# The 32 whole value rows of the second tile, spread among its 96 partial ones

## The reference

```python
cand_idx = i_top[..., 0, :, None] * PEER_KEYS + i_top[..., 1, None, :]   # expert = first key * 128 + second key
best, pos = lax.top_k(cand, PEER_TOPK)          # 16 experts for each of 8 heads and each token
act = gelu(einsum('ckd,cd->ck', expert_u[idx], xc))
out = einsum('ck,ckd->cd', gate * act, expert_v[idx])   # 128 value rows for each token, summed with weights
return rms_norm(h + out, final_norm)
```

## Time and profile before

| | us |
|---|---|
| timed runs | 2013.01, 2016.02, 2017.6 |
| span of the profiled execution, first to last instruction | 2008.7 |
| time around the span in that execution | not in the trace |
| PE, DVE, POOL busy | 1770.1, 1368.9, 1040.7 |
| mean DMA rate over the span | 322 GB/s |

### The profile page before, as it was taken

How to read it: one execution, slowest core, us unless ns; L and a number is a source line. 1 busy time by engine, 2 the same in 40 slices (tenths; PEclk the granted TensorE clock), 3 DMA queues, 4 the chain that set the end, 5 groups by cost and what they waited for, 6 DMA issues and landing times.

```text
span 2008.7 us, 18796 instructions
## 1 busy us (share of the span) xinstructions
PE 1770.1 (88%) x6283; PEld 1122.4 (56%) x6283; DVE 1368.9 (68%) x2191; ACT 574.5 (29%) x1037; POOL 1040.7 (52%) x643
## 2 busy tenths in 40 slices
PE   7999999999999999875565578898887899999996
PEld 6888888888888898622222233344333554444442
DVE  5463453233334338999889887787888888888956
ACT  5445464345543520210111132233313740000001
POOL 5443343444332413575555565465555668877732
PEclk9999999999999999887778899999998899999999
DMA  8986454665555679999999999999999999999997
GB/s 211 241 177 148 142 189 152 192 196 180 169 164 173 204 263 403 384 411 420 418 419 417 402 420 419 414 413 414 403 415 391 401 369 408 409 414 386 409 421 308
DMA packets 157641, 647.28 MB, mean 322 GB/s; under 512 B 25894, under 2 KB 31086, under 8 KB 95598
## 3 DMA queue, kind: packets, MB, share of 16 engines
q0 software_dynamic: 73728, 450.98, 55.2%
q1 hardware_dynamic: 83824, 195.16, 30.9%
HBM read 729.91 MB, written 2.10 MB: 364 GB/s over the span
## 4 chain that ended last, share of the span: by engine, by line
PE 52%; DMA 18%; DVE 13%; issue 9%; POOL 7%; POOLq 0%; ACT 0%; DVEq 0%; SPq 0%; ACTq 0%
DMA u_ring<-in_peer_u_dram,idx 10%; PE acc L1583 10%; PE acc L1585 10%; PE acc L1584 10%; PE misc L1967 8%; PE acc L1967 8%; DMA u_high<-in_peer_u_dram,idx 3%; DVE u_ring L1425 3%; DMA u_mid<-in_peer_u_dram,idx 3%; DVE u_ring L1423 3%; POOL u_ring L595 3%; POOL v_high L602 1%; POOL u_mid L595 1%; DVE u_mid L1425 1%; DVE u_mid L1423 1%
## 5 line engine op out<-in xcount | busy, mean ns | idle before, releaser
L553 POOL TENSOR_TENSOR w_lo<-raw,w_hi 128x1024 fp32r<-128x1024 f32 x112 | 276.3, 2467 | 421.0 <-ACT w_hi L677 420.7
L1583 PE MATMUL acc<-w_hi,t_hi 128*128 128x512 f32 x896 | 355.0, 396 | 0.0
L1585 PE MATMUL acc<-w_hi,t_lo 128*128 128x512 f32 x896 | 349.3, 390 | 0.0
L1584 PE MATMUL acc<-w_lo,t_hi 128*128 128x512 f32 x896 | 348.9, 389 | 0.0
L1025 DVE TENSOR_TENSOR w_lo<-raw,w_hi 128x1024 fp32r<-128x1024 f32 x112 | 158.4, 1415 | 265.7 <-ACT w_hi L677 265.6
L595 POOL DMA_INDIRECT u_ring<-in_peer_u_dram,idx x160 | 210.2, 1314 | 249.0 <-DVE dots L1425 195.1
L677 ACT ACTIVATE w_hi<-raw 128x1024 fp32r<-128x1024 f32 x224 | 237.0, 1059 | 330.8 <-PE acc L1585 281.1
L1932 PE MATMUL misc<-v_high,diag 128*128 128x512 f32 x368 | 203.7, 705 | 87.0 <-DMA v_high<-in_peer_v_dram,idx 84.2
L1932 PE MATMUL misc<-v_low,diag 128*128 128x512 f32 x368 | 191.7, 670 | 79.1 <-DMA v_low<-in_peer_v_dram,idx 79.1
L1423 DVE CUSTOM_DVE_ANT_0 u_ring<-u_ring,hn 128x1024 f32<-128x1024 f32 x160 | 195.8, 1224 | 72.5 <-DMA u_ring<-in_peer_u_dram,idx 65.8
L1425 DVE CUSTOM_DVE_ANT_0 u_ring<-u_ring,hn 128x1024 f32<-128x1024 f32 x160 | 195.3, 1221 | 0.0
(11 more groups left out here) (286 smaller groups left out, 2433.4 us busy)
## 6 DMA issues: line engine op xcount, KB each, us to landing
u_ring<-in_peer_v_dram SPq DMA_DIRECT2D x48, 1024.0 KB, 8.9
raw<-in_w_in_dram SPq DMA_DIRECT2D x64, 512.0 KB, 7.0
raw<-in_xattn_wk_dram SPq DMA_DIRECT2D x32, 512.0 KB, 4.6
raw<-in_xattn_wv_dram SPq DMA_DIRECT2D x32, 512.0 KB, 3.9
raw<-in_w_out_dram SPq DMA_DIRECT2D x32, 512.0 KB, 4.7
raw<-in_xattn_wq_dram SPq DMA_DIRECT2D x32, 512.0 KB, 4.9
raw<-in_xattn_wo_dram SPq DMA_DIRECT2D x32, 512.0 KB, 4.8
praw<-in_peer_wq_dram SPq DMA_DIRECT2D x24, 512.0 KB, 8.6
```

What stands on the lines that cost most here:

```text
L553: nc.gpsimd.tensor_tensor(w_lo[:, j % RING, :, :], raw[:, j % RING, :, :], w_hi[:, j % RING, :, :].bitcast(F32), ALU.subtract).then_inc(lo ...
L1583: nc.tensor.matmul(o, xh, w_hi[:, s, kk, :], start=first, stop=False)
L1584: nc.tensor.matmul(o, xh, w_lo[:, s, kk, :], start=False, stop=False)
L1585: ins = nc.tensor.matmul(o, xl, w_hi[:, s, kk, :], start=False, stop=last)
```

## The change

`late_row(m)` maps the place m in the order of work to a row as it was numbered before. The first four places stay partial (`SPREAD = 4`); after them the 32 whole rows stand evenly among the partial ones: at places 4, 7, 11, 15, 19, 23, 27, 31, 35, 38, and so on to 112, 116, 120 and 124. Among themselves the partial rows keep their order, and so do the whole ones. Slots, waits for slots, and the places that PE takes go by the place m as before. DVE waits for its own last weights once, before place 3's add.

```diff
+        SPREAD = 4
+        PARTIAL = TOP * (PH - WHOLE)
+        def whole_before(m):
+            return max(0, min(TILE0 - PARTIAL, ((m - SPREAD) * (TILE0 - PARTIAL) + TILE0 - SPREAD - 1) // (TILE0 - SPREAD)))
+        def late_row(m):
+            w = whole_before(m)
+            return PARTIAL + w if whole_before(m + 1) > w else m - w
+        assert sorted(map(late_row, range(TILE0))) == list(range(TILE0))
...
-                gather_v(TILE0 + m, v_slot(slot), late_landed[slot])
+                gather_v(TILE0 + late_row(m), v_slot(slot), late_landed[slot])
...
-                                     scale=low_wts[:, PH + m // TOP, m % TOP:m % TOP + 1]).then_inc(diag_ready, 1)
+                                     scale=low_wts[:, PH + late_row(m) // TOP, late_row(m) % TOP:late_row(m) % TOP + 1]).then_inc(diag_ready, 1)
...
                 if m == 3:
                     weights(GROUPS - 1)
+                    dve.wait_ge(wts_ready, GROUPS)
```

More of the change, by code:

```diff
@@ L1463, in add_values @@
                 at = 0 if m < SHARED else CW
-                nc.vector.scalar_tensor_tensor(y_sum[:, 1, at:], v_slot(late_slot(m))[:, at:], low_wts[:, PH + m // TOP, m % TOP:m % TOP + 1],
+                nc.vector.scalar_tensor_tensor(y_sum[:, 1, at:], v_slot(late_slot(m))[:, at:], low_wts[:, PH + late_row(m) // TOP, late_row(m) % TOP:late_row(m) % TOP + 1],
                                                (y_sum if m else h)[:, 1, at:], ALU.mult, ALU.add).then_inc(v_added, 1)
@@ L1479, in add_last @@
                     cols = slice(i * CW, (i + 1) * CW)
-                    nc.vector.scalar_tensor_tensor(y_sum[:, 1, cols], v_slot(late_slot(m))[:, cols], low_wts[:, PH + m // TOP, m % TOP:m % TOP + 1],
+                    nc.vector.scalar_tensor_tensor(y_sum[:, 1, cols], v_slot(late_slot(m))[:, cols], low_wts[:, PH + late_row(m) // TOP, late_row(m) % TOP:late_row(m) % TOP + 1],
                                                    y_sum[:, 1, cols], ALU.mult, ALU.add).then_inc(y_added, 1)
```

## The result

The changed kernel takes 2028.84 us (median of 4 runs, 2025.64 to 2031.79) where the kernel before took 2014.97 in the runs beside it. The medians differ by 13.9 us; the ratio formed from all these runs is 1.0064, interval 1.0051 to 1.0078, so the kernel is slower, clear of the noise. The forecast was slower, 2023, with a range to 2029: the side was right and the loss about twice the +7 forecast.

What follows compares the result with a forecast made beforehand. Bound before: PE's dense tiles with DMA full to about 1965, then the last row's gather. DVE's extra tail adds gave +8.5 (middle of +6.7 and +10.2), less 1.5 coming back, +7: 2016 + 7 = 2023, range 2012 to 2029.

Steps and rivals of the forecast that it cites:

- late issue: Rival, chance 0.07: in the tail, gathers waiting for PE's slots miss DVE's gaps, up to 9.8 us more, 2033.
- landing times: Dense stage: rows ahead priced at 3.86 us a megabyte, place 107 landing at 1963, end +10.2 us.
- the upper of the two counts of rows: Rows left at 1961: 17.5, with partial rows at 0.586 MB, 5.8 more than before for DVE.
- The wait: DVE's wait after its last weights, paid once: 0.1 us, bounds 0 and 0.2.
- Whole rows 4 and 7 ahead of the dense stage: Before 1638 us: 0.77 MB more gathered, at most 1.9 us, taken as 0 since PE does not wait for DMA.
- The order of bytes: At 1961, the same bytes left are 16.2 to 17.5 mixed rows, not 11.75: +6.7 to +10.2 us.
- What comes back: Light rows' stretch, 1831 to 1870: whole rows between may fill 1.2 MB; -1.5 us, bounds 0 and -4.1.
- The hole of the earlier trace: Light rows at 1831 to 1870 us: DMA at 376 GB/s against 406 on average, 1.2 MB short.
- No new wait in the tail: From about 1963 to its last add DVE waits for no DMA, 47 us; rows arrive every 1.7 us.
- Gather issue: POOL in the tail: one gather per add, 2.45 us, with 9 slots in hand; taken as 0.
- Evens out: Rival, chance 0.21: hole filled in full and slowest engine's lag shrinks; 4.2 us, covered by 4.1 of waiting: 2016.
- faster: Rival, chance 0.16: mixed stream runs at 422 GB/s throughout, row 113 landed by 1963, end -4.1 or more: 2011.

Runs made afterwards that it cites:

- even gathers: Kernel before, with partial rows except the first in each slot gathered as 1280 columns for all tokens, none skipped: 2009.33 us, ratio 0.9975.

## Why the prediction was right, and where its size was off

The mechanism that the prediction gave came: more rows are left to DVE when the dense tiles end, DVE adds them without a wait for DMA, the last gathers land before they are needed, and the end is DVE's and no longer a gather's. That 2028.84 lies inside the range is in part luck. It is above the 2019 to 2026 that the forecast gave by itself; of the cases weighed only late issue, which did not happen, lay beyond 2026. In the profiles the loss is +15.9 to the last add, 9 more than +7: 4.0 from landing times, 1.8 from a wait of PE that no term held, 1.5 that were expected back and did not come, and 1.7 because the upper of the two counts of rows held.

- *The wait*, 0.1: right, 2015.94 by itself.
- *Whole rows 4 and 7 ahead of the dense stage*, 0: right, PE idles 2.6 us as before.
- *The order of bytes*: right. By 1967 the same 131.29 MB are in, and 17.25 rows are left where 16.2 to 17.5 were forecast.
- *Landing times*: the direction right and the size short. I priced the rows ahead at 3.86 us a megabyte, from a stretch of whole rows at 422 GB/s, and had place 107 at 1963. It came at 1967.0 (by the clock of before), and place 104 only at 1959.6. That stretch moved 364 GB/s and less. The byte count could not show this: it counts packets, and a row counts for DVE only when its last packet is in.
- *What comes back*, -1.5: wrong in kind, for these gathers. The hole of the earlier trace rows was filled, as two of the rivals have it, but nothing came back: by 1967 the sum of bytes is the same. The hole is not a place in the order of rows that whole ones can fill; it moved to the last 50 us before the dense end, where it costs rows in the tail. With this term at 0 the sum is +8.5, and its upper end +10.2.
- *No new wait in the tail*: DMA was never waited for there, as forecast, but PE was, for 2.35 us: +1.8. I had looked at ACT only for the shape of its instructions and not for the order in which it makes the four matrices.
- *Gather issue*, 0: right. In the tail POOL issued one gather per add, and DVE never waited for it, so the rival of late issue did not happen. The prediction's "the trace does not agree" goes further than its rows: the gather reads its list of indices (`idx`), which lies in SBUF, so its 2.15 us beside the adds may come from that read; no run tells the two apart.
- *Evens out* and *faster* needed the mixed stream to hold the whole rows' rate to the end. It came near it, 407 to 420 GB/s in the windows from 1669 us on, only to about 1919 us.

## What to carry to other kernels

When a stage ends with work that only one engine can do, count the pieces left at that moment, not the bytes: the light pieces belong early, the heavy ones last. Price a moved transfer by a stretch with the same kind of transfers beside it, and ask whether a hole in the rate belongs to the place or to the transfers themselves; if to the transfers, moving them moves it. And when an end moves, look at what other engines' fixed order ties to it.

## What the runs showed of the hardware

PE's clock falls with its waits in the tail. The granted clock was 0.64 in 1970 to 1980 us of the changed kernel, in which PE idles 8.01 us, and 0.81 in 2010 to 2020. Eight matmuls that take 3.60 us at full clock took 6.73 behind 5.99 us of idling; the granted clock beside them was 0.51, which is the lower of the two levels, 1.2 instead of 2.4 GHz (window, busy times, then the clock). So this wait of PE cost itself and 3.1 us more. Before, behind 1.24 us of idling, the eight took 3.67.

```profile
2007.70:2014.00 6.30, 6.30 (x8) 2.69 (x9) 4.30 (x2) 0.71 (x3) 0.00 (x0) 0.51 0.79 306
```

A DMA share near 1.0 is not a full rate of bytes. In the lightest rows the kernel before ran at 376 GB/s with a share of 0.98, and the one with even gathers in the same order, in the same stretch, at 418 with 1.02:

```profile
1831.00:1870.00 39.00, 39.00 (x93) 17.24 (x92) 33.29 (x15) 0.00 (x0) 30.24 (x14) 1.00 0.98 376
1831.00:1870.00 39.00, 39.00 (x93) 17.23 (x92) 37.09 (x16) 0.00 (x0) 34.12 (x17) 1.00 1.02 418
```

Over the whole dense stage it is 406 GB/s and 415, in 323 us from 1637 us on, with 2842 packets under 512 bytes for 6709:

```profile
DMA packets 23214, 133.92 MB, mean 415 GB/s; under 512 B 2842, under 2 KB 2842, under 8 KB 13594
```
